# Two RMS norms in a row, after the attention block and before the next block: both taken from sums of squares of the same tensor, gathered beside the output product

## The reference, cut to what matters

```
# end of the first block
h_lat = h_lat + gate[:, None] * y_lat        # y_lat: output product of the attention
x = rms_norm(h_lat, final_norm_g)

# start of the second block
h = _rms_norm(x, g_pre_mix)
proj = h @ w_in                              # c_q is its first 384 columns
...
x = x + _rms_norm(merged @ w_o, g_post_mix)  # x is needed again here

def rms_norm(x, g):                          # eps 1e-6 in both
    y = x * lax.rsqrt(jnp.mean(x * x, axis=-1, keepdims=True) + NORM_EPS)
    return y * g
```

## Time and profile before

| | |
|---|---|
| profiled execution, its own time | 3263.36 us |
| its span | 3261.5 us |
| median of three timed executions | 3266.5 us |
| TensorE busy | 2970.4 us (91%) |
| VectorE busy | 1322.7 us (41%) |
| ScalarE busy | 976.0 us (30%) |
| mean granted TensorE clock | 0.967 |
| HBM read and written | 182.79 MB and 11.53 MB |

### The profile page before, as it was taken

How to read it: one execution, slowest core, us unless ns; L and a number is a source line. 1 busy time by engine, 2 the same in 40 slices (tenths; PEclk the granted TensorE clock), 3 DMA queues, 4 the chain that set the end, 5 groups by cost and what they waited for, 6 DMA issues and landing times.

```text
span 3261.5 us, 38098 instructions
## 1 busy us (share of the span) xinstructions
PE 2970.4 (91%) x15878; PEld 1879.8 (58%) x15878; DVE 1322.7 (41%) x2814; ACT 976.0 (30%) x2457; POOL 64.7 (2%) x52
## 2 busy tenths in 40 slices
PE   7799999999999769979999789999898888799998
PEld 3567777778777555645554335464554433488743
DVE  3357475575665534322222233322243210577501
ACT  1335546356454430012232222212233301211101
POOL 0000000000000000000000000000000000000000
PEclk9899999999999889999999999999999999899999
DMA  5101101101012027101000120111111012122111
GB/s 201 40 10 55 44 21 45 55 20 41 20 44 80 20 88 296 52 33 52 26 26 33 35 90 26 52 61 69 65 52 77 4 74 107 48 83 98 54 71 44
DMA packets 76508, 196.78 MB, mean 60 GB/s; under 512 B 56144, under 2 KB 61008, under 8 KB 64944
## 3 DMA queue, kind: packets, MB, share of 16 engines
q1 hardware_dynamic: 49648, 172.48, 14.3%
q10 hardware_dynamic: 26688, 21.86, 2.1%
HBM read 182.79 MB, written 11.53 MB: 60 GB/s over the span
## 4 chain that ended last, share of the span: by engine, by line
PE 79%; DVE 9%; ACT 6%; DMA 4%; issue 1%; ACTq 0%; SPq 0%; DVEq 0%
PE ps L968 13%; PE ps L1649 8%; PE ps L1061 5%; PE ps L1586 5%; PE ps L1464 5%; PE ps L1281 3%; PE ps L1596 3%; PE ps L1468 2%; PE ps L1024 2%; ACT arena L1686 2%; PE ps L1348 2%; PE ps L958 2%; PE ps L1363 2%; PE ps L1282 2%; ACT arena L1687 2%; DVE arena L2388 2%
## 5 line engine op out<-in xcount | busy, mean ns | idle before, releaser
L1686 ACT ACTIVATE arena<-ps 64x64 f32<-64x64 f32 (+8 forms) x952 | 313.8, 358 | 1013.8 <-PE ps L968 355.1
L968 PE MATMUL ps<-arena 128*128 128x512 f32 (+1 forms) x976 | 421.2, 591 | 46.1 <-DVE arena L2277 15.2
L968 PEld LDWEIGHTS ps<-arena 128*128 128x128 f32 x976 | 188.0, 194 | 273.4 <-issue 229.8
L1024 PE MATMUL ps<-arena 128*128 128x512 f32 x512 | 264.7, 598 | 1.7 <-DVE arena L2277 1.7
L1649 PE MATMUL ps<-arena 128*128 128x256 f32 x1176 | 254.5, 378 | 0.0
L1649 PEld LDWEIGHTS ps<-arena 128*128 128x128 f32 x1176 | 222.3, 189 | 32.5 <-issue 0.5
L1586 PE MATMUL ps<-arena 128*128 128x512 f32 x384 | 173.5, 604 | 20.0 <-issue 20.0
L1464 PE MATMUL ps<-arena 128*128 128x512 f32 x384 | 179.8, 596 | 5.1 <-ACT arena L2033 3.1
L1687 ACT ACTIVATE arena<-ps,arena 128x128 f32<-128x128 f32 x544 | 156.7, 380 | 84.5 <-PE ps L1179 43.3
L1061 PE MATMUL ps<-arena 128*128 128x256 f32 x768 | 180.3, 388 | 0.0
L1025 PEld LDWEIGHTS ps<-arena 128*128 128x128 f32 x512 | 97.0, 189 | 124.6 <-issue 124.6
(11 more groups left out here) (295 smaller groups left out, 4152.1 us busy)
## 6 DMA issues: line engine op xcount, KB each, us to landing
arena<-in_ada_w SPq DMA_DIRECT2D x12, 2048.0 KB, 17.0
arena<-in_w_up SPq DMA_DIRECT2D x11, 2048.0 KB, 7.7
arena<-in_w_dil SPq DMA_DIRECT2D x9, 2048.0 KB, 7.5
arena<-in_w_dn SPq DMA_DIRECT2D x8, 2048.0 KB, 10.4
arena<-in_w_gate SPq DMA_DIRECT2D x6, 2048.0 KB, 12.3
arena<-in_w_down SPq DMA_DIRECT2D x8, 1408.0 KB, 5.9
arena<-in_att_in SPq DMA_DIRECT2D x5, 2048.0 KB, 7.7
arena<-in_w_z SPq DMA_DIRECT2D x8, 1024.0 KB, 4.9
```

What stands on the lines that cost most here:

```text
L968: m = e.matmul(out, w[:, (k * m_tiles + x) * 128:(k * m_tiles + x) * 128 + 128], src(k), start=k == 0, stop=k == nk - 1)
L1024: e.matmul(ps[:, b1, :], w, uT[:, k * T_ALL + 256:(k + 1) * T_ALL], start=k == 0, stop=k == 7)
L1686: return e.activation(out, x, ACT.Copy)
```

## The change

h's squares are taken tile by tile beside the output product. ScalarE squares each tile of h as soon as it is in place, twice: once as it is, once with scale `final_g` (so (h·g1)²). The first tile's squares go straight into `sumA` and `sumB`; VectorE adds those of tiles 1 to 6 to them, those of tile n-1 behind the residual of tile n. TensorE multiplies `sumA`, `sumB` and the two squares of tile 7 with ones: four products in banks 4 and 5 in place of sixteen. Then one chain gives both roots: r1 = (mean(h²)+eps)^-0.5 (`r5`), r1² (`r1sq`), r2 = (mean((h·g1)²)·r1² + eps)^-0.5, and `r12` = r1·r2. VectorE writes `hn` first, straight from h with the gain `gp` = g1·g2 and the root `r12`, and `X` behind it. TensorE's `cq` waits tile by tile. The buffers of the sums and roots lie in `X`, which is written only after `pre_x` 7.

```diff
+        sumA, sumB, sqB5, sqB6, r1sq, r2, r12 = (X[:, a * 512:a * 512 + 512] for a in range(7))
+        squares2 = [[sq5[0], sqB5], [sq5[1], sqB6]]
+        gp = X[:, 3584:3592]
...
# TensorE
-            mean_square("fin", 8, 512, 4, sq5)
-            mean_square("pre", 8, 512, 4, sq5)
-            e.wait_ge(*at("pre_x", 7))
+            take_banks(4, 5)
+            for v, total in enumerate((sumA, sumB)):
+                e.wait_ge(*at("fin_add", 6, v))
+                e.matmul(ps[:, 4 + v, :], ones, total, start=True, stop=False)
+            for v in range(2):
+                e.wait_ge(*at("fin_sq", 7, v))
+                e.matmul(ps[:, 4 + v, :], ones, squares2[1][v], start=False, stop=True).then_inc(*mark("fin_ms", v))
+            leave_banks(("fin_r", 0), 4)
+            leave_banks(("fin_t",), 5)
             e.wait_ge(*here("w_cq", 0))
+            def fresh(k):
+                e.wait_ge(*at("pre_x", k))
+                return hk(k)
...
-                product("cq", n, slab("w_cq", 0), 3, n, 8, hk, n)
+                product("cq", n, slab("w_cq", 0), 3, n, 8, fresh, n)
...
# ScalarE
-            mean_square("fin", 8, 512, 4, sq5, lambda k: hT[:, k * T_ALL + 256:(k + 1) * T_ALL], r5, 1024.0,
-                        lambda k: ("att_out_ev", 7))
-            mean_square("pre", 8, 512, 4, sq5, lambda k: X[:, k * 512:(k + 1) * 512], r5, 1024.0,
-                        lambda k: ("fin_x", 7))
+            for n in range(8):
+                o = hT[:, n * T_ALL + 256:(n + 1) * T_ALL]
+                e.wait_ge(*at("att_out_ev", n))
+                for v in range(2):
+                    if n >= 3:
+                        e.wait_ge(*at("fin_add", n - 2, v))
+                    e.activation(squares2[n % 2][v] if n else (sumA, sumB)[v], o, ACT.Square,
+                                 scale=V("final_g", n, n + 1) if v else 1.0).then_inc(*mark("fin_sq", n, v))
+            e.wait_ge(*at("fin_ms", 0))
+            e.activation(r1sq, ps[:, 4, :], ACT.Ln, bias=eps, scale=1.0 / 1024.0).then_inc(*mark("fin_r", 0))
+            e.wait_ge(*at("fin_r", 0))
+            e.activation(r5, r1sq, ACT.Exp, scale=-0.5).then_inc(*mark("fin_r", 1))
+            e.wait_ge(*at("fin_r", 1))
+            e.activation(r1sq, r1sq, ACT.Exp, scale=-1.0).then_inc(*mark("fin_r", 2))
+            e.wait_ge(*at("fin_t"))
+            e.activation(r2, r2, ACT.Ln, bias=eps, scale=1.0 / 1024.0).then_inc(*mark("pre_r", 0))
+            e.wait_ge(*at("pre_r", 0))
+            e.activation(r2, r2, ACT.Exp, scale=-0.5).then_inc(*mark("pre_r", 1))
...
-                        lambda k: ("cq_ev", k), ("pre_x", 7))
+                        lambda k: ("cq_ev", k), ("fin_x", 7))
...
# VectorE
                 e.scalar_tensor_tensor(o, ps[:, n % 4, :], modv(1, 16 + n, 0), o, MUL, ADD).then_inc(*mark("att_out_ev", n))
+                if n == 0:
+                    e.tensor_tensor(gp, V("final_g"), V("pre_mix"), MUL).then_inc(*mark("gp"))
+                if n >= 2:
+                    for v, total in enumerate((sumA, sumB)):
+                        e.wait_ge(*at("fin_sq", n - 1, v))
+                        if n > 2:
+                            e.wait_ge(*at("fin_add", n - 2, v))
+                        e.tensor_tensor(total, total, squares2[(n - 1) % 2][v], ADD).then_inc(*mark("fin_add", n - 1, v))
...
-            normed("fin", 8, X, lambda k: hT[:, k * T_ALL + 256:(k + 1) * T_ALL], V("final_g"))
-            normed("pre", 8, hn, lambda k: X[:, k * 512:(k + 1) * 512], V("pre_mix"))
+            e.wait_ge(*at("fin_ms", 1))
+            e.wait_ge(*at("fin_r", 2))
+            e.tensor_tensor(r2, ps[:, 5, :], r1sq, MUL).then_inc(*mark("fin_t"))
+            e.wait_ge(*at("pre_r", 1))
+            e.tensor_tensor(r12, r2, r5, MUL).then_inc(*mark("fin_r12"))
+            e.wait_ge(*at("fin_r12"))
+            e.wait_ge(*at("gp"))
+            for to, x_tag, gain, root in ((hn, "pre_x", gp, r12), (X, "fin_x", V("final_g"), r5)):
+                if to is X:
+                    e.wait_ge(*at("pre_x", 7))
+                for k in range(8):
+                    e.scalar_tensor_tensor(to[:, k * 512:(k + 1) * 512], hT[:, k * T_ALL + 256:(k + 1) * T_ALL],
+                                           gain[:, k:k + 1], root, MUL, MUL).then_inc(*mark(x_tag, k))
```

## The result

Six timed executions of the changed kernel beside six of the kernel before: median 3247.05 us (3245.9 to 3250.6) against 3266.94 us (3265.04 to 3267.77). The ratio is 0.9941, with a 95% interval of 0.993 to 0.9951: 19.9 us less, faster by 0.6%. The forecast was 3242.7 us, 23.8 us less, with a range up to 3247.5. The gain has the sign of the forecast and stops 3.9 us short of it; the forecast lies just outside of what the ratio's interval allows (0.993 of 3266.5 is 3243.6).

A forecast was written before the change was run, and what follows sets the result against it. Most of the program was taken as bound by TensorE's products (79% of the chain), with TensorE standing during the norms. A 23.0 us earlier `cq` plus 0.8 us of clock gave 23.8 us less, 3242.7 us, range 3238 to 3247.5.

The forecast's parts named there:

- What goes: Between last residual and `cq`: all 32.14 us of norm work goes; squares and additions beside the output product cost nothing.
- The new ladder: Seven steps from last residual to `cq`, from sums through roots to first `hn` tile: 9.2 us; `cq` 23.0 us earlier.
- some 3.7: Expected sign in the changed profile: four products with ones within some 3.7 us behind the last residual.
- The clock behind the gap: TensorE idles 4.8 us ahead of `cq`; lower clock then costs 1.7 us against 2.46 before, 0.8 us more gained.
- the 1.00 of the earlier trace: Granted clock that the prediction said the 1.5 us between output product and first product with ones left at 1.00.
- The cover of the copies: ScalarE's late `cq` copies: two done by 1841.9, `cq` ends at 1844.2; cover 2.3 us, 0.6 if the clock stays high.
- The stretch: From the end of the output product to the end of `cq`; before 1811.68 to 1867.95, forecast to end at 1844.2.
- What stands behind: Angles, copies, DMAs and everything after `cq`: costed at nothing, no event behind 1868 tied to wall clock, shift kept.
- 2 us either way: Forecast's uncertainty for the program's later gaps, which fall elsewhere against the chip's own rhythms: some 2 us.
- The part ahead: Program up to the end of the output product, the same in both kernels; 1811.68 us in the profile before.
- signs of being wrong: `cq` starting after 1824, a new copy or cosine in the chain after `cq`, or later stages moving by other than 24 us.
- the clock that stays high: Rival: no lower clock behind the new gap ahead of `cq`; 25.5 us gained, 3241.0 us; chance 0.15.

The follow-up runs named there:

- warm: Changed kernel plus five products with ones into an unread bank behind the norm's four, filling TensorE's idle time ahead of `cq`; 3246.18 us.
- tight: Changed kernel with additions of tile n-1 ahead of the residual of tile n, and the squared root's Exp ahead of the Exp for r1; 3244.98 us.
- late_angles: Changed kernel plus seven VectorE additions (5.0 us) ahead of the angles; no whole time given, norm of `cq` started 36.56 us behind the output product, `ckv` ended 4.0 us later.

## Why the prediction was off

By its own steps:

- *What goes* (32.14 us): right. The output product was not held up in any of the runs.
- *The new ladder* (9.95 us from the end of the product to `cq`): measured 10.19. The steps' durations were off by 0.1 at most; the rest is signals. The four products with ones were done 4.35 us behind the last residual. The prediction's own steps give 4.37; the "some 3.7" among its signs didn't follow from them.
- *The clock behind the gap* (1.7 us lost): 1.71, and `warm` shows that it is the clock. That the number fits is partly luck. The row nearest in length gave it, yet `tight` idled 4.40 us and lost 3.05, more than the largest loss that the prediction allowed (2.46). Two readings were loose: the 1.00 of the earlier trace rows is the clock in that gap and not behind it (behind it, it was 1.00 too, in both kernels), and the change shortens one gap and takes the one from 1820.72 to 1828.33 away. The Trainium skill's advice against such gaps (TensorE: Matmul & The Clock Gate, Why this matters for your kernels) held. In this case's trace 5.07 us of idleness was followed by a granted clock of 0.57.
- *The cover of the copies* (2.3 us): 2.48, and `late_angles` shows both that it is there and what lies beyond.
- The stretch was forecast at 32.5 us and took 32.78.
- *What stands behind*: **this step failed**. It said that no event behind 1868 is tied to the clock on the wall, "so the shift should be kept to the end". 2.9 of the 23.5 us were given back some 477 us later and beyond, by no engine and no transfer that the change touches, but by TensorE's clock. I had put the later idle times down as 2 us either way, a scatter around zero. It is no scatter in the profiles: the two of either kernel agree there to 0.13 us, since this part hangs on how the program lies against the rhythm. The kernel before had 0.96 and 0.71 there, in rows that I used for another purpose. They could have warned that the low stretch depends on where the idle time lies. That 0.4 us of shift decides it, and that it costs about 3 us, only the runs showed.
- *The part ahead* is the same program in both kernels and scatters over 6 us (1811.68 to 1817.67 in 14 profiles). Of the 23.8 us forecast, 0.3 are missing in the stretch and 2.9 behind it, which leaves 20.6. The medians of the two sets (19.9 and 23.0 less) lie around that, closer than the scatter of the part ahead.

Two of the prediction's signs of being wrong appeared. `cq` started after 1824, at 1827.86, but only by the part ahead: counted from the output product it is 10.19 us, and in the second profile it started at 1822.53. And the end of the program moved by 14.6 us in the first pair of profiles and 20.6 in the second, not by 24. That was the sign that mattered, since behind `cq` the loss repeats.

Of the rivals none came true. The nearest in kind was the clock that stays high, and it was a different idle time that mattered.

Still open: why the DMA at 958 us is slow in five of the profiles, with the low clock 36 us further on; no run was made for it. And what the later waits for weights add to the 1.4 us was read, not tested.

## What to carry to other kernels

Gather a norm's sums beside the product that feeds it (6.35 us here for one norm, 10.4 for the sums of both), derive the roots of two norms in a row in one chain, and let the tensor that TensorE waits for be written first (6.2 us): all of it is work on engines that stood idle. Check an expected gain by the stretch between two fixed events, and only then by the whole time: with parts ahead and behind that move by 3 to 6 us, single times hid a stretch 6 us longer. And when a shift passes over later idle times of TensorE, like that of 5.09 us here, give the clock there a term of its own, of either sign.

## What the hardware showed that I had not expected

- Some work costs nothing, and a little can cost much: with 2.58 us of added products behind `ckv` the changed kernel's part behind was no longer (1396.28 against 1396.45 and 1396.58), and 0.43 us of them made that of the kernel before 3.4 us longer.
- The same idle time of 5.09 us was followed by 5.14 us at a granted clock of 0.67 to 0.71 in eight profiles and of 0.50 in six. The Trainium skill (TensorE: Matmul & The Clock Gate, HAM clock gate) says that the monitor runs free of the kernel. The traces agree, in that the changes of the clock lie differently against the program's start in each profile, and add that two profiles of one kernel nevertheless repeat.
- An idle time of 5.07 us ahead of `cq` cost 1.71 us (changed kernel), one of 4.40 us cost 3.05 us (`tight`), and one of 0.77 us nothing (`warm`): the loss doesn't follow the length of the idle time alone.
- ScalarE's Square of 128x512 with a scale from SBUF, in a pair with one without, took 1.24 us against 1.15 for two without.
